# Eight attention gate tiles computed ahead of the attention instead of six, and a new table of gate products per attention step

## What is computed

```python
def gated_mixer_block(u, w_in, pool_w_group, pool_scale, w_branch_pool, w_branch_attn, w_out):
    proj = u @ w_in                  # [xp | q | k | v | gate_logits]
    ...
    y_pool = causal_pool_mixer(xp, pool_w_group, pool_scale) @ w_branch_pool
    o_sb = stick_breaking_attention(q, k, v).transpose(0, 2, 1, 3).reshape(b, s, SB_WIDTH)
    y_sb = o_sb @ w_branch_attn
    g = jax.nn.sigmoid(gate_logits.astype(jnp.float32)).astype(u.dtype)
    g_pool, g_sb = jnp.split(g, 2, axis=-1)
    return (g_pool * y_pool + g_sb * y_sb) @ w_out

def stick_breaking_attention(q, k, v):
    for blk in range(s_len // Q_BLOCK):        # 8 heads of width 64, 8 blocks of 128 rows
        z = jnp.einsum('bhqd,bhkd->bhqk', qb, kb).astype(jnp.float32) * scale
        mask = kpos < qpos
        log_beta = jax.nn.log_sigmoid(z)
        log_1m_beta = jnp.where(mask, jax.nn.log_sigmoid(-z), 0.0)
        log_a = log_beta + lax.cumsum(log_1m_beta, axis=3, reverse=True) - log_1m_beta
        a = jnp.where(mask, jnp.exp(log_a), 0.0)
        outs.append(jnp.einsum('bhqk,bhkd->bhqd', a.astype(vb.dtype), vb))
```

## Time and profile before

| | us |
|---|---|
| median of three runs | 1911.35 |
| the profiled execution, its own time | 1911.22 |
| its span | 1909.3 |
| TensorE (PE) busy | 1899.8 |
| VectorE (DVE) busy | 1370.5 |
| ScalarE (ACT) busy | 799.4 |
| GpSimd (POOL) busy | 135.0 |

### The profile page before, as it was taken

How to read it: one execution, slowest core, us unless ns; L and a number is a source line. 1 busy time by engine, 2 the same in 40 slices (tenths; PEclk the granted TensorE clock), 3 DMA queues, 4 the chain that set the end, 5 groups by cost and what they waited for, 6 DMA issues and landing times.

```text
span 1909.3 us, 24938 instructions
## 1 busy us (share of the span) xinstructions
PE 1899.8 (100%) x8998; PEld 1591.0 (83%) x8998; DVE 1370.5 (72%) x1686; ACT 799.4 (42%) x1177; POOL 135.0 (7%) x157
## 2 busy tenths in 40 slices
PE   9999999999999999999999999999999999999998
PEld 9888888888888888888888888898888888888886
DVE  6977777784565786469677768889777777755655
ACT  7423232323434544324577762473323232334344
POOL 1000000000000200000145420010000000000001
PEclk9999999999999999999999999999999999999999
DMA  5456654558676733423866557634455445677665
GB/s 165 151 198 228 225 178 142 198 189 307 209 237 204 199 110 133 133 72 106 242 175 176 138 163 261 185 128 134 165 162 179 167 152 163 222 262 239 205 194 201
DMA packets 258419, 348.24 MB, mean 182 GB/s; under 512 B 29344, under 2 KB 161184, under 8 KB 255008
## 3 DMA queue, kind: packets, MB, share of 16 engines
q1 hardware_dynamic: 258016, 346.62, 56.2%
q10 hardware_dynamic: 320, 0.52, 0.1%
HBM read 233.83 MB, written 112.99 MB: 182 GB/s over the span
## 4 chain that ended last, share of the span: by engine, by line
PE 97%; DVE 1%; DMA 1%; ACT 0%; issue 0%; SPq 0%; POOL 0%; POOLq 0%; ACTq 0%
PE bank L1271 41%; PE bank L1327 8%; PE bank L1328 8%; PE bank L1329 8%; PE bank L1380 8%; PE bank L1520 7%; PE bank L1223 3%; PE bank L1430 2%; PE bank L1458 2%; PE bank L1488 2%; PE bank L1590 2%; PE bank L1609 1%; PE bank L1608 1%; PE bank L1198 1%; PE bank L1575 1%; PE bank L1573 1%
## 5 line engine op out<-in xcount | busy, mean ns | idle before, releaser
L2270 DVE TENSOR_TENSOR dn_lo<-dn_lo_raw,dn_hi 128x1024 fp32r<-128x1024 f32 x149 | 181.7, 1223 | 150.9 <-ACT dn_hi L1793 150.3
L1271 PE MATMUL bank<-hi_t,wa_lo 128*128 128x512 f32 x656 | 252.8, 389 | 0.0
L1271 PE MATMUL bank<-lo_t,wa_hi 128*128 128x512 f32 x656 | 252.8, 389 | 0.0
L1271 PE MATMUL bank<-hi_t,wa_hi 128*128 128x512 f32 x656 | 252.7, 389 | 0.0
L1793 ACT ACTIVATE dn_hi<-dn_lo_raw 128x1024 fp32r<-128x1024 f32 x149 | 157.9, 1061 | 220.2 <-DMA dn_lo_raw<-act_dram 220.2
L1327 PE MATMUL bank<-dn_hi 128*128 128x512 f32 x596 | 232.5, 390 | 0.0
L1329 PE MATMUL bank<-dn_lo,dn_hi 128*128 128x512 f32 x596 | 231.9, 389 | 0.0
L1328 PE MATMUL bank<-dn_hi,dn_lo 128*128 128x512 f32 x596 | 231.9, 389 | 0.0
L1271 PE MATMUL bank<-hi_b,wa_hi 128*128 128x512 f32 x492 | 190.4, 389 | 0.0
L1271 PE MATMUL bank<-lo_b,wa_hi 128*128 128x512 f32 x492 | 190.4, 389 | 0.0
L1271 PE MATMUL bank<-hi_b,wa_lo 128*128 128x512 f32 x492 | 190.4, 389 | 0.0
(11 more groups left out here) (275 smaller groups left out, 3846.0 us busy)
## 6 DMA issues: line engine op xcount, KB each, us to landing
wa_lo_raw<-in_ffn_w_gate_up_dram SPq DMA_DIRECT2D x87, 512.0 KB, 5.0
dn_lo_raw<-act_dram SPq DMA_DIRECT2D x149, 256.0 KB, 4.3
act_dram<-g SPq DMA_DIRECT2D x44, 512.0 KB, 4.4
wd_t<-in_ffn_w_down_dram SPq DMA_DIRECT2D x44, 512.0 KB, 6.7
act_dram<-s_of SPq DMA_DIRECT2D x88, 256.0 KB, 6.4
wd_dram<-wd_t SPq DMA_DIRECT2D x22, 1024.0 KB, 5.9
dn_lo_raw<-wd_dram SPq DMA_DIRECT2D x85, 256.0 KB, 3.3
dn_lo_raw<-in_ffn_w_down_dram SPq DMA_DIRECT2D x64, 256.0 KB, 3.0
```

What stands on the lines that cost most here:

```text
L1271: last = nc.tensor.matmul(acc, lhs, rhs, start=n == 0 and i != 2 and i < 5, stop=n == 11, skip_group_check=True)
L2270: return nc.vector.tensor_tensor(dst, raw, hi.bitcast(f32), ALU.subtract)
```

## The change

Eight attention gate tiles are made ahead (`EARLY` = 8), so `MIX_UNITS` has eight units and `GATE_UNITS` four, all of pooling gates: 16 banks, 384 matmuls. Since there is one unit more, the second `unit_quad` and all mixing units swap their halves of PSUM: both quads now use banks 0 to 3, the first mixing unit banks 4 to 7, so that the last one ends in the same banks as before. The parities of the branch weights' slots are written as `KT % 2` and `j % 2`, which are the same slots that the branch used. `SHARE` has new weights.

```diff
-EARLY = 6
+EARLY = 8
...
-SHARE = {7: 8, 6: 14, 1: 14, 0: 11, 5: 10, 4: 11, 3: 12, 2: 12}
+SHARE = {7: 16, 6: 8, 1: 23, 0: 4, 5: 13, 4: 1, 3: 15, 2: 12}
...
@@ unit_quad
-                    if not fresh:
-                        pe.wait_ge(tr_free, 4 * NT)
+                    wait_bank(b, q)
...
-                        last = products(bank[:, b if fresh else 4 + b, :], par, ab, lambda kt: u_hi[:, kt, cols],
+                        last = products(bank[:, b, :], par, ab, lambda kt: u_hi[:, kt, cols],
...
@@ mix_unit (TensorE; ScalarE and VectorE read the same banks)
-                s = (b + NM + 1) % 2
+                s = (b + 1) % 2
                 for i in range(7):
                     place, hi, lo, (kind, slot) = PRODUCTS[i]
-                    if b < 2 and i in (0, 1, 3, 4):
-                        wait_bank(place, Q_A[b] + 1)
+                    if b == 0 and i == 0:
+                        pe.wait_ge(tr_free, 4 * NT)
+                    if b == 1 and i in (0, 1, 3, 4):
+                        wait_bank(place, Q_A[1] + 1)
...
@@ branch weights
-                branch_tile(j, (U_C + j) % 2, j // 2)
+                branch_tile(j, j % 2, j // 2)
```

More of the change, by code:

```diff
@@ L1950, in take_first @@
                 act.wait_ge(acc_ready, 4 * Q_A[m] + b + 1)
-                nc.scalar.activation(ring_hi[n % 3][:, th * HALF:(th + 1) * HALF], bank[:, 4 * m + b, :], ACT.Copy,
+                nc.scalar.activation(ring_hi[n % 3][:, th * HALF:(th + 1) * HALF], bank[:, b, :], ACT.Copy,
                                      scale=1.0 if ab else QSCALE).then_inc(ev_hi, 1)
@@ L1974, in mix_first @@
                 act.wait_ge(mb_prod, 7 * b + 1)
-                nc.scalar.activation(mix_dst(b, 0, 0), bank[:, 4 * ((b + NM + 1) % 2), :], ACT.Copy).then_inc(mb_copied, 1)
+                nc.scalar.activation(mix_dst(b, 0, 0), bank[:, 4 * ((b + 1) % 2), :], ACT.Copy).then_inc(mb_copied, 1)
             def mix_second(b):
@@ L1981, in mix_second @@
                     act.wait_ge(mb_add, 5 * b)
-                nc.scalar.activation(mid[:, :], bank[:, 4 * ((b + NM + 1) % 2), :], ACT.Copy).then_inc(mb_copied, 1)
+                nc.scalar.activation(mid[:, :], bank[:, 4 * ((b + 1) % 2), :], ACT.Copy).then_inc(mb_copied, 1)
             def mix_post(b, a, th, adds):
@@ L2238, in outputs_hi @@
                 nc.scalar.activation(o_piece(u_hi, i), o_piece(xu, i), ACT.Copy).then_inc(o_hi, 1)
-            act.wait_ge(raw_in[U_C % 2], 32 * (U_C // 2 + 1))
+            act.wait_ge(raw_in[KT % 2], 32 * (U_C // 2 + 1))
             act.wait_ge(gate_ready, GATE_LAST[NG - 2] + 1)
-            nc.scalar.activation(w_hi[:, U_C % 2, 0, 0:BR], w_raw[:, U_C % 2, 0, 0:BR], ACT.Copy).then_inc(whi, 1)
+            nc.scalar.activation(w_hi[:, KT % 2, 0, 0:BR], w_raw[:, KT % 2, 0, 0:BR], ACT.Copy).then_inc(whi, 1)
             for i in range(len(O_PARTS)):
@@ L2249, in split_branch @@
             def split_branch(j):
-                act.wait_ge(raw_in[(U_C + j) % 2], 32 * ((U_C + j) // 2 + 1))
+                act.wait_ge(raw_in[j % 2], 32 * ((U_C + j) // 2 + 1))
                 act.wait_ge(acc_ready, 4 * Q_C + 2 * (j - 1))
-                nc.scalar.activation(w_hi[:, (U_C + j) % 2, 0, 0:BR], w_raw[:, (U_C + j) % 2, 0, 0:BR], ACT.Copy).then_inc(whi, 1)
+                nc.scalar.activation(w_hi[:, j % 2, 0, 0:BR], w_raw[:, j % 2, 0, 0:BR], ACT.Copy).then_inc(whi, 1)
             for n in range(1, KT):
@@ L2719, in take_first @@
                 cols = slice(th * HALF, (th + 1) * HALF)
-                nc.vector.scalar_tensor_tensor(out=ring_lo[(2 * m + ab) % 3][:, cols], in0=bank[:, 4 * m + b, :], scalar=1.0 if ab else QSCALE,
+                nc.vector.scalar_tensor_tensor(out=ring_lo[(2 * m + ab) % 3][:, cols], in0=bank[:, b, :], scalar=1.0 if ab else QSCALE,
                                                in1=ring_hi[(2 * m + ab) % 3][:, cols].bitcast(f32), op0=ALU.mult,
@@ L2784, in mix_c11 @@
                 dst = mix_dst(b, 0, 0)
-                nc.vector.tensor_tensor(dst, bank[:, 4 * ((b + NM + 1) % 2) + 1, :], dst, ALU.add).then_inc(mb_add, 1)
+                nc.vector.tensor_tensor(dst, bank[:, 4 * ((b + 1) % 2) + 1, :], dst, ALU.add).then_inc(mb_add, 1)
             def mix_c22(b, part):
-                dst, s = mix_dst(b, 1, 1), (b + NM + 1) % 2
+                dst, s = mix_dst(b, 1, 1), (b + 1) % 2
                 if part:
@@ L2805, in mix_c12 @@
                 dve.wait_ge(mb_prod, 7 * b + 6)
-                nc.vector.tensor_tensor(mix_dst(b, 0, 1), bank[:, 4 * ((b + NM + 1) % 2) + 2, :], mid[:, :], ALU.add).then_inc(mb_add, 1)
+                nc.vector.tensor_tensor(mix_dst(b, 0, 1), bank[:, 4 * ((b + 1) % 2) + 2, :], mid[:, :], ALU.add).then_inc(mb_add, 1)
             def mix_c21(b):
                 dve.wait_ge(mb_prod, 7 * b + 7)
-                nc.vector.tensor_tensor(mix_dst(b, 1, 0), bank[:, 4 * ((b + NM + 1) % 2) + 3, :], mid[:, :], ALU.add).then_inc(mb_add, 1)
+                nc.vector.tensor_tensor(mix_dst(b, 1, 0), bank[:, 4 * ((b + 1) % 2) + 3, :], mid[:, :], ALU.add).then_inc(mb_add, 1)
             def mix_out(b, a, th, posts):
@@ L3110, in _ @@
                     dve.wait_ge(whi, U_C + 1)
-                    nc.vector.tensor_tensor(flat(w_lo[:, U_C % 2, 0, 0:BR]), flat(w_raw[:, U_C % 2, 0, 0:BR]),
-                                            flat(w_hi[:, U_C % 2, 0, 0:BR]).bitcast(f32), ALU.subtract).then_inc(wlo, 1)
+                    nc.vector.tensor_tensor(flat(w_lo[:, KT % 2, 0, 0:BR]), flat(w_raw[:, KT % 2, 0, 0:BR]),
+                                            flat(w_hi[:, KT % 2, 0, 0:BR]).bitcast(f32), ALU.subtract).then_inc(wlo, 1)
             outputs_lo(len(O_PARTS) - 1)
@@ L3145, in split_branch @@
                 dve.wait_ge(whi, U_C + j + 1)
-                dst, raw, hi = (flat(w[:, (U_C + j) % 2, 0, 0:BR]) for w in (w_lo, w_raw, w_hi))
+                dst, raw, hi = (flat(w[:, j % 2, 0, 0:BR]) for w in (w_lo, w_raw, w_hi))
                 nc.vector.tensor_tensor(dst, raw, hi.bitcast(f32), ALU.subtract).then_inc(wlo, 1)
```

## The result

The changed kernel takes 1922.97 us (median of four runs, 1921.38 to 1924.77) against 1911.32; the ratio is 1.006 with a 95% interval of 1.0048 to 1.0073. It is 11.6 us slower. The forecast was 1920, with 1916 to 1924 for the likeliest case. The profiled execution took 1924.5 us, 13.3 more than the one before.

What follows compares the result with a forecast made beforehand. TensorE's own instructions were taken as the bound, others mattering only where it waits. -2.9 (work) + 8.8 (chains) + 2.3 (start) + 0.7 (end) = +8.9 us, so 1920 us; likeliest case 1916 to 1924, bounds 1905 and 1925.

Steps and rivals of the forecast that it cites:

- The work: TensorE: 96 gate products leave the attention (22.0 us), one mixing unit of 84 matmuls comes (19.0 us); net -2.9 us.
- The chains: Attention, `turn` to a later `weigh`: TensorE waits for `at_lo`, 10.9 us in four kinds, 2.1 already there; +8.8 us.
- block 5 to 4: Transposes to `weigh` load, 2.54 us on other engines; three or four gate products left, waits 0.63 or 0.40; 3.7 us.
- block 6 to 0: Path with VectorE's longest scan, 4.74 us against TensorE's 4.40; seven waits of 0.34, three quarters 1.9; 4.3 us.
- block 4 to 2: Nine gate products left cover the bare path; quarters in steps 20, 28 and 36 add 0.6 each; 1.8 us.
- The quarters: A weight quarter split by VectorE inside a path from transposes to `weigh` lengthens TensorE's wait by about 0.6 us.
- The start: First `weigh`: TensorE arrives 2.7 us earlier, first quarter's data no earlier, so it waits to 943.8; +2.3 us.
- The end: Behind the last head: two `weigh` and one branch product with one or two fewer gate products ahead; +0.7 us.
- A: Attention: chains shrink with the schedule, no new wait; 1906 to 1908.5 us; chance 0.06.
- D: Second quad, ahead of the mixing units, waits for its PSUM banks despite 11 us of cover; chance under 0.01.
- B: Attention: other engines catch up during waits, leaving only bare chain parts; +2 us, 1913.5; chance 0.18.
- C: Attention: VectorE becomes the bound through contention, from 0.6 us per head; 1925 us and more; chance 0.10.

Runs made afterwards that it cites:

- six tiles with a number for each step: Kernel before the change (six gate tiles ahead) with 69 per-step gate-product counts, sum 480, in place of the share table; 1909.57 us, ratio 0.9991.
- later profile: The changed kernel run again, unchanged, five runs; median 1921.67 us, ratio 1.0054, profiled execution 1921.99 us.
- half scan: Changed kernel with VectorE's scan of each block 7 tile run over only the first 512 of 1024 keys; 1918.51 us, ratio 1.0036.
- eight tiles, a number for each step: Changed kernel with the first attention weight quarter split later and a gate-product count for each step, sum 384; 1914.27 us, ratio 1.0018.
- the same with the changed kernel's end: Changed kernel, first quarter split later, per-step counts: last five steps as in the changed kernel, first 64 rearranged; 1912.62 us, ratio 1.0007.
- The old table: Changed kernel, still eight gate tiles ahead, with SHARE put back to its weights from before the change; 1921.73 us, ratio 1.0054.
- the new table with six tiles: Kernel before the change, still six gate tiles ahead, with only the changed kernel's SHARE weights; 1914.31 us, ratio 1.0016.
- the late quarter: Changed kernel with its first attention gate unit's quarters split at 40, 52, 64, 76 gate products instead of 26, 42, 58, 74; 1918.05 us, ratio 1.0037.
- the fitted table: Changed kernel with SHARE weights fitted to the four kinds of chain, same number of gate products in a head; 1924.59 us, ratio 1.0070.

## Why the prediction was right, and where its terms were off

**The work, -22.0 + 19.0.** Right: 19.1 us for 84 matmuls, 18.98 at the attention's start.

**The chains, +8.8.** Right in mechanism, place and nearly in size. By kinds, in us of waits in the load rows:

| | forecast | measured |
|---|---|---|
| block 5 to 4 | 3.7 | 4.9, 7 times |
| block 6 to 0 | 4.3 | 5.1, 7 times |
| block 4 to 2 | 1.8 | 2.8, 5 times |
| block 7 to 6 and value tiles | 1.1 | 0.4, once |
| sum | 10.9 | 13.2 |

Less the 2.1 of before that is +11.1 in the rows. Less of it is in the time, since a load normally leads its matmul by up to 0.23 us and a wait eats that lead first. How much, the runs tell. The attention without a wait is 214.04 us for 480 products (the profile of six tiles with a number for each step), and so 214.04 - 96 x 0.229 = 192.1 for 384, an estimate. What each profile has above that, beside its waits in the load rows and what the clock lost:

| | above it, us | waits + clock, us | waits | hidden in each, us |
|---|---|---|---|---|
| before | 1.6 | 3.0 | 9 | 0.15 |
| changed, first profile | 17.8 | 20.7 + 1.7 | 27 | 0.17 |
| changed, later profile | 15.7 | 19.9 | 27 | 0.16 |
| half scan | 11.3 | 14.8 | 21 | 0.17 |
| eight tiles, a number for each step | 8.9 | 13.0 | 25 | 0.16 |
| the same with the changed kernel's end | 6.0 | 9.9 | 24 | 0.16 |

The old table (0.16), the new table with six tiles (0.16) and the late quarter (0.16) give the same; only the fitted table differs (0.12). So in nine of the ten profiles the waits and the clock account for the whole time, once some 0.16 us are taken off each wait. The chains' 11.1 us of added rows, in 20 waits for 7, are worth 9.0 us. The prediction took the rows at full value; this error and the kinds' excess nearly cancelled, so that its +8.8 came out closer than its terms: that much was luck.

Most of the first three rows' excess of 3.0 us is in weight quarters that the prediction did not count. It had three in block 0's path and three in block 2's. One more is in block 2's (0.59 us, step 4), and two are in block 4's, where it had none. The one in the fifth head:

```profile
1059.29 0.67 DVE L3078 TENSOR_TENSOR w_lo<-w_raw,w_hi 128x512 fp32r<-128x512 f32 x1
1059.88 1.15 DVE L3066 TENSOR_TENSOR at_lo<-bank,at_hi 128x512 fp32r<-128x512 f32 x2
...
1061.08 0.19 PEld L1609 LDWEIGHTS bank<-at_hi,v_w 128*128 128x128 f32 x1 [1.23 <-DVE at_lo L3066]
```

The wait is 1.23 us where it is 0.65 without a quarter; the one in the second head makes 0.77 of 0.43. In the fourth head ScalarE's part of a quarter (0.68 us at 1029.79) stands ahead of `at_hi`: block 0's wait is 0.76 us instead of 0.40. Together that is 1.9 us. Another 0.4 is a value tile's conversion, which the prediction had in the last row and which shows in block 2's. And `turn` has a wait of its own (0.24 us at 1035.14 in the fourth head, ahead of the place shown above), for which the prediction had no term; it starts the second part of the transposes later and makes the wait behind them 0.50 instead of the 0.40 forecast.

**The quarters, 0.6 each.** Right: 1.05 us with one, 0.40 without.

**The start, +2.3.** The step that failed. The prediction let the quarter's data land when they did before, put `at_lo` of the second tile about 0.5 us earlier, and had the only wait at the first `weigh`. Measured are 3.2 us at the transposes of the second tile, 0.5 at the first `weigh`, 1.4 for q_st and 1.7 of clock, some 6.3 us of time in the first profile (less 0.16 for each wait) and 3.6 in the later one. Two things were overlooked: that `turn` needs the bank emptied three chunks earlier, so that the late quarter blocks TensorE already there; and that the quarter's data may come later. SyncE's issue of them, before and after:

```profile
930.19 0.64 SPq L818 DMA_DIRECT2D w_raw<-in_w_in_dram  x1
```

```profile
949.83 0.54 SPq L818 DMA_DIRECT2D w_raw<-in_w_in_dram  x1
```

The issue is 19.64 us later, 0.7 more than the attention's start; from issue to use it is 8.8 us before, 11.6 in the first profile and 9.8 in the later one. Why the transfer took longer stays open; the runs vary in it with the same program.

**The end, +0.7.** Right: 0.6 more at the last two `weigh` and 0.7 at the first branch product, 1.1 us after the loads' lead.

**The sum.** -2.9, +9.0 for the chains, +0.1 for `turn`'s own wait, +6.3 for the start, +1.1 for the end: 13.6 for the 13.3 between the two profiled executions; with the later profile's start and end it is 11.1, for 10.8 between that execution and the one before. The start's term was 4.0 us too small in the first profile and 1.3 in the later one, and that is most of what the measured times have over the forecast's 1920.

**The rivals.** A (no new waits) and D fall by the waits' rows. B (half of it) falls too for this table; a better spread of the same products does come out near the 1913.5 that it named, for another reason than the one it gave. C (contention that lengthens block 0's chain by 0.6 us in each head) gets no support: without a quarter that wait is 0.40 us where bare durations gave 0.34. By the 216 ns that the Trainium skill (TensorE: Matmul & The Clock Gate, section Back-to-back issue gap) gives for an isolated matmul of 512 columns, the net would be 2.6 us instead of 2.9, an estimate; the trace disagrees with it here too, 152.48 / 672 = 0.2269 us.

## What to carry to other kernels

In a pipeline where one engine is always busy, its filler work is what covers the chains of the others. Before moving filler away to save its own cost, count for each handshake how much stands between its two ends, and what else each engine does between them; here 22 us of products left, 2.9 net, and 14 to 16 came back as waits. Spread filler by step, against all orders at once (copies, quarters, banks to be freed, the last output), since a table fitted to some of the waits moved them to the others.

## What the runs showed of the hardware

A wait can cost more than its length, in the clock behind it. After TensorE's load had waited 3.2 us at the transposes, the granted clock was 0.56 for 3.8 us (1.2 GHz for nearly all of it); after 4.7 us ahead of the branch it was 0.53 for 3.6 us, and with the old table after 2.6 us it was 0.50 in the 2 us behind. After 1.4 and 1.3 us (the changed kernel's later profile), and after the 2.2 us for q_st's data with the late quarter, it stayed at 1.00.

And a wait can cost less than its length: some 0.16 us of each wait in a load's row is not in the time (0.15 to 0.17 in nine profiles, 0.12 in one), which fits a load that leads its matmul by up to 0.23 us.

The same program's first weight quarter took 11.6 us from issue to use in one profile and 9.8 in another, at a DMA share near 1 in both (1.07 and 1.08).
